# Full-height operands for two score products, closer softmax steps in layer B, a queries' product between two keys' products, and latent queries rotated by GpSimd

## The chip, the cores and the metric

The program runs on one core of one Trainium2 chip. Its metric is the device time of one execution in microseconds (us). The kernel before took 1611.77 us, the median of 3 runs (1610.45 to 1612.25). The engines are TensorE (PE, with its weight loads as PEld), VectorE (DVE), ScalarE (ACT), GpSimd (POOL) and SyncE (SP), which issues the loads.

## The reference, cut to what matters

Two blocks run one after the other over 512 tokens of width 1024. The first has a layer A (a stabilised mLSTM beside attention over a memory) and a layer B (latent attention with 8 heads beside memory attention); the second has differential attention, cross-attention over a second memory (layer D here) and an MLP. Two places of it matter here. In layer A the decay of a pair of tokens is exp(d - m_t), where m_t is the running maximum of a token:

```python
d = b[..., :, None] - b[..., None, :] + ib[..., None, :]
m_t = jnp.maximum(inter, jnp.max(d, axis=-1))
p = jnp.einsum("bhtd,bhsd->bhts", qb, kb) * jnp.exp(d - m_t[..., None])
```

In layer B each of 8 heads has queries and keys of 128 plain and 64 rotary components, normalised together; the rotary keys are shared by the heads but for each head's norm:

```python
q = (rmsnorm(q_lat, q_lat_g) @ w_q_up).reshape(bsz, s, B_HEADS, QK_HEAD)
q = rmsnorm(q, q_gain)
q = jnp.concatenate([q[..., :QK_NOPE], rope(q[..., QK_NOPE:], positions)], axis=-1)
...
sc = jnp.einsum("bqhd,bkhd->bhqk", q[:, qs:ke], k[:, :ke]) * scale
p = jax.nn.softmax(jnp.where(k_chunk <= q_chunk, sc, -jnp.inf), axis=-1)
```

In layer D, cross-attention, queries are `h @ w_cq` (512 tokens), keys and values `mem_n @ w_ckv` (256 tokens), with 4 heads of 256.

## The kernel before, in words

Every weight product is computed in three matmuls a tile, of a high and a low fp32r half of each operand (hi*hi, hi*lo, lo*hi). Weights come in chunks of 256 rows: SP loads a chunk into one of two raw slots (`fetch`), ACT copies its high half and DVE subtracts to get the low half (`split`), into one of three split slots. A product has 4 output tiles (banks 0 to 3), each evicted by ACT or DVE (`ev`). The attention scores, transposes and values are plain fp32 matmuls, in banks 4 to 7.

One list of steps sets the order on all engines. `order_of_work` calls `p.product(...)` for the products, and hangs side work (softmax units, transposes, values) into two lanes. `Plan.advance` takes the head of a lane between two product rows once a counted clock, which sums formula costs of PE's work, has moved on by that group's `lag` since the lane's last group. `rounds` makes the groups of an attention: group n holds the turn-over (transposes) of unit n-2, the normalising of unit n-1 and the scores of unit n, and `exp` of unit n stands in a group of its own after `wait`. Each engine's program walks the same list and runs the part that is its own, strictly in order.

The names that the change touches:

- `asc` is a score unit of layer B, one head and one block of 128 queries, 32 in all, 8 each of 128, 256, 384 and 512 keys. It is a matmul over the 128 plain components (L1404), one over the 64 rotary components (L1405; a head's half of the pair's rows is taken by `hs`) and a bf16 matmul that adds the mask (L1221). `atp` transposes the probabilities (L1205), `aval` multiplies them with the values (L1420). `msc`, `mtp`, `mval` are the same for the memory attention, 16 units in layer B.
- `hsc` is a score step of layer A, 16 in all: the running maximum is spread to 128 rows by a product with a 4-row selector (L1350), a mask is added, then come queries times keys (L1356, L1357).
- `latents(q)` prepares two heads: the products `kvB` and `quB`, then side steps `prep0` to `prep6`. `prep0`, `prep1`, `prep3`, `prep4` transpose the plain parts, `prep5` the rotary keys and `prep6` the rotary queries. DVE rotates the queries in `prep4` and `prep5`, with 7 instructions (recorded at the helper line L1927), and ACT moves the turned result of `prep6` from its bank into `peT`.
- GpSimd adds up the squares for norms (L2460), takes reciprocal roots (L2451) and does little else in layer B.
- `ckD0`, `ckD1` are the keys' products of layer D (256 tokens), `cqD0`, `cqD1` the queries', `cvD` the values'. `outB0`, `outB1` are the output product of layer B; its last tiles of input are the results of heads 4 to 7.

## Time and profile before

| what | value |
|---|---|
| median of 3 runs | 1611.77 us (1610.45 to 1612.25) |
| the profiled execution | 1605.89 us |
| its span, first to last instruction | 1604.1 us |
| mean granted TensorE clock | 0.993 of full speed |
| PE busy | 1552.2 us (97%) |
| DVE busy | 890.2 us (55%) |
| ACT busy | 705.5 us (44%) |
| POOL busy | 192.1 us (12%) |

Places in the span are given in us from its start. Layer B's attention lies at about 550 to 804 us, layer A's `hsc` steps at 168 to 390 us, layer D's products from 1068 us. A duration in a row of the timeline is from the first start to the last end of the instructions merged in it. Matmuls overlap in their records, so what a matmul costs TensorE is read from one start to the next. An fp32 product is recorded as two matmuls ("x2"), an fp32r product as one.

### The profile page before, as it was taken

What the parts mean: (1) busy time and instruction counts of PE and PEld (TensorE: products, weight loads), DVE (VectorE), ACT (ScalarE), POOL (GpSimd) and SP (SyncE); (2) the same over time, 40 slices, a digit from 0 to 9 for tenths busy, and PEclk for the clock granted to TensorE, in tenths of its full rate; (3) what the DMA queues carried; (4) which work ended last, traced back from release to release, by engine and by line L of the source; (5) the groups of instructions that cost most, each with busy time, mean ns of one, the idle gap of its engine ahead of it and who ended that gap; (6) DMA issues with size and microseconds to landing.
All of it is one profiled execution on the core that took longest, in us unless ns stands there. A gap on an engine that the chain in (4) does not pass through costs nothing.

```text
span 1604.1 us, 19197 instructions
## 1 busy us (share of the span) xinstructions
PE 1552.2 (97%) x7128; PEld 1239.7 (77%) x7128; DVE 890.2 (55%) x1775; ACT 705.5 (44%) x1607; POOL 192.1 (12%) x157
## 2 busy tenths in 40 slices
PE   7999999999999999999899999999999999999997
PEld 5887777777897877766478878688777888888886
DVE  6467485656465567556448557664455534444343
ACT  6544353333355666555334444442344333333241
POOL 3202020202120000000014004320001100000001
PEclk9999999999999999999999999999999999999998
DMA  5522122323424222121123321234322333333321
GB/s 191 158 74 72 53 80 66 92 66 118 125 67 143 81 62 61 49 71 42 40 79 120 92 67 55 65 105 120 99 84 79 95 103 93 101 96 93 105 93 65
DMA packets 89068, 141.04 MB, mean 88 GB/s; under 512 B 6416, under 2 KB 36496, under 8 KB 88976
## 3 DMA queue, kind: packets, MB, share of 16 engines
q1 hardware_dynamic: 88256, 139.02, 28.5%
q8 instruction: 56, 0.92, 0.2%
q10 hardware_dynamic: 720, 0.81, 0.1%
q14 instruction: 36, 0.29, 0.1%
HBM read 137.71 MB, written 2.10 MB: 87 GB/s over the span
## 4 chain that ended last, share of the span: by engine, by line
PE 78%; DVE 9%; ACT 5%; issue 3%; POOL 3%; DMA 2%; SPq 0%; POOLq 0%; ACTq 0%; DVEq 0%
PE banks L1242 16%; PE banks L1244 16%; PE banks L1243 16%; PE banks L1247 6%; PE banks L1249 6%; PE banks L1248 6%; PE banks L1205 2%; DVE sb_w_split L1927 2%; DVE sb_arena L1936 2%; ACT sb_junk L1512 2%; PE banks L1420 1%; PE banks L1405 1%; PE banks L1368 1%; ACT sb_w_split L1544 1%; DVE sb_arena L1927 1%
## 5 line engine op out<-in xcount | busy, mean ns | idle before, releaser
L1927 DVE TENSOR_TENSOR sb_w_split<-sb_raw,sb_w_split 128x512 fp32r<-128x512 f32 (+4 forms) x530 | 338.7, 681 | 359.8 <-ACT sb_w_split L1544 359.1
L1544 ACT ACTIVATE sb_w_split<-sb_raw 128x512 fp32r<-128x512 f32 (+4 forms) x530 | 288.2, 592 | 425.3 <-PE banks L1244 309.5
L1242 PE MATMUL banks<-sb_actA,sb_w_split 128*128 128x512 f32 x672 | 275.7, 410 | 0.3 <-ACT sb_arena L1604 0.3
L1244 PE MATMUL banks<-sb_actA,sb_w_split 128*128 128x512 f32 x672 | 262.7, 391 | 0.0
L1243 PE MATMUL banks<-sb_actA,sb_w_split 128*128 128x512 f32 x672 | 261.8, 390 | 0.0
L1242 PE MATMUL banks<-sb_actB,sb_w_split 128*128 128x512 f32 (+1 forms) x640 | 248.8, 389 | 4.2 <-DVE sb_actB L1927 2.2
L1244 PE MATMUL banks<-sb_actB,sb_w_split 128*128 128x512 f32 (+1 forms) x640 | 242.9, 379 | 0.0
L1243 PE MATMUL banks<-sb_actB,sb_w_split 128*128 128x512 f32 (+1 forms) x640 | 242.7, 379 | 0.0
L1247 PE MATMUL banks<-sb_w_split,sb_actA 128*128 128x512 f32 (+1 forms) x384 | 153.5, 400 | 12.6 <-DVE sb_w_split L1927 9.2
L1249 PE MATMUL banks<-sb_w_split,sb_actA 128*128 128x512 f32 (+1 forms) x384 | 149.3, 389 | 0.0
L1248 PE MATMUL banks<-sb_w_split,sb_actA 128*128 128x512 f32 (+1 forms) x384 | 149.0, 388 | 0.0
L1242 PEld LDWEIGHTS banks<-sb_actA,sb_w_split 128*128 128x128 f32 x672 | 126.4, 188 | 27.6 <-issue 2.9
L1244 PEld LDWEIGHTS banks<-sb_actA,sb_w_split 128*128 128x128 f32 x672 | 126.1, 188 | 27.6
L2460 POOL TENSOR_TENSOR sb_arena<-sb_arena 128x512 f32<-128x512 f32 x43 | 63.4, 1475 | 697.5 <-ACT sb_arena L1585 695.0
L1243 PEld LDWEIGHTS banks<-sb_actA,sb_w_split 128*128 128x128 f32 x672 | 126.5, 188 | 24.7 <-issue 0.7
L1242 PEld LDWEIGHTS banks<-sb_actB,sb_w_split 128*128 128x128 f32 x640 | 121.0, 189 | 27.7 <-DVE sb_actB L1927 2.7
L1243 PEld LDWEIGHTS banks<-sb_actB,sb_w_split 128*128 128x128 f32 x640 | 120.9, 189 | 22.9 <-issue 1.4
L1244 PEld LDWEIGHTS banks<-sb_actB,sb_w_split 128*128 128x128 f32 x640 | 120.7, 189 | 22.8
L2451 POOL TENSOR_TENSOR sb_small<-sb_small,sb_cons 128x4 f32<-128x4 f32 (+3 forms) x30 | 42.1, 1403 | 589.7 <-DVE sb_small L1933 589.7
L1247 PEld LDWEIGHTS banks<-sb_w_split,sb_actA 128*128 128x128 f32 x384 | 72.9, 190 | 26.9 <-issue 12.9
L1247 PE MATMUL banks<-sb_w_split,sb_actB 128*128 128x512 f32 (+2 forms) x208 | 81.5, 392 | 2.8 <-DVE sb_w_split L1927 1.7
L1249 PEld LDWEIGHTS banks<-sb_w_split,sb_actA 128*128 128x128 f32 x384 | 72.9, 190 | 14.5
(206 smaller groups left out, 2061.4 us busy)
## 6 DMA issues: line engine op xcount, KB each, us to landing
sb_raw<-in_a_w_in SPq DMA_DIRECT2D x66, 256.0 KB, 3.0
sb_raw<-in_w_up SPq DMA_DIRECT2D x32, 512.0 KB, 3.6
sb_raw<-in_w_down SPq DMA_DIRECT2D x32, 512.0 KB, 3.7
sb_raw<-in_w_in SPq DMA_DIRECT2D x24, 512.0 KB, 3.6
sb_raw<-in_mem_w_kv SPq DMA_DIRECT2D x16, 512.0 KB, 3.8
sb_raw<-in_w_ckv SPq DMA_DIRECT2D x16, 512.0 KB, 3.7
sb_raw<-in_a_w_in SPq DMA_DIRECT2D x15, 512.0 KB, 3.8
sb_raw<-in_a_w_out SPq DMA_DIRECT2D x12, 512.0 KB, 3.9
```

What stands on the lines that cost most here:

```text
L1205: t = pe.op.transpose(v.ps[0:rows, place.bank, n * P:(n + 1) * P], block, v.ident)
L1242: pe.op.matmul(out, hi[:, cs], x.hi(k), start=i == 0, stop=False)
L1243: pe.op.matmul(out, hi[:, cs], x.lo(k), start=False, stop=False)
L1244: t = pe.op.matmul(out, lo[:, cs], x.hi(k), start=False, stop=last_i)
L1247: pe.op.matmul(out, x.hi(k)[:, cs], hi, start=i == 0, stop=False)
L1248: pe.op.matmul(out, x.hi(k)[:, cs], lo, start=False, stop=False)
L1249: t = pe.op.matmul(out, x.lo(k)[:, cs], hi, start=False, stop=last_i)
L1512: t = act.op.activation(v.junk[:, 0:src.shape[-1]], src, ACT.Square, accum_out=out)
L1544: act.op.activation(hi[:, cs], raw[:, cs], ACT.Copy).then_inc(act.mark(m("w_hi"), 2 * n + part + 1), 1)
L1927: dve.op.tensor_tensor(out, a, b, op).then_inc(dve.mark(*mark) if mark else dve.tick(), 1)
L2451: pool.op.tensor_tensor(v.stat(root, n), v.stat(mean, n), v.con("minus_half", 0, n), ALU.pow).then_inc(m.at("rstd", step)[0], 1)
L2460: pool.op.tensor_tensor(total, total, v.square_of(norm, n)[1], ALU.add).then_inc(pool.mark(signal, value), 1)
```

## The change: what it does, and the diff

Seven edits, in three sorts. Full height: `m_rows` is a whole tile that GpSimd zeroes once and whose first 4 rows are `neg_m`, and L1350's product reads 128 rows of it. The rotary queries of each head go into a tile of their own, `q_pe`, whose other 64 rows are zeroed by GpSimd, so that the rotary product reads 128 rows; ACT's move in `prep6` becomes two of 64 rows each. Order: the `lag` and `wait` of the rounds in layer B are shorter, `prep6` stands further behind `prep5`, `ckD1` moves behind `cqD0`. Engine: the 7 instructions of `prep4` and `prep5` go from DVE to GpSimd.

```diff
@@ order_of_work: mla, mem_b, latents
-               lag=1400, wait=1000)
+               lag=1300, wait=1000)
...
-               [("hnscale", "mqB"), ("hnt", "mk1", 3)], [("silu", f"mzB{h0 // 2}", 1)], lag=1600, wait=1200)
+               [("hnscale", "mqB"), ("hnt", "mk1", 3)], [("silu", f"mzB{h0 // 2}", 1)], lag=1300, wait=1000)
...
-            p.side(1, [("asc", 2 * q - 3, TT - 1)] if q >= 2 and n == 0 else (), (f"prep{n}", q), lag=4000 if n in (0, 6) else 2600)
+            after = [("asc", 2 * q - 3, TT - 1)] if q >= 2 and n == 0 else [("ysplit", "yB", 3)] if (q, n) == (3, 4) else ()
+            p.side(1, after, (f"prep{n}", q), lag={0: 4000, 6: 6500}.get(n, 2600))
...
-    p.product("ckD1")
     p.rings = [(4, 5), (6, 7)]
     for g in range(2):
-        p.product(f"cqD{g}", [("nrow", "d")])
+        p.product(f"cqD{g}", [("nrow", "d")], first=False)
+        if g == 0:
+            p.product("ckD1")
@@ Views
-        self.neg_m = self.arena[0:4, at.at:at.at + SEQ]
-        at.take(SEQ)
+        self.m_rows = at.take(SEQ)
+        self.neg_m = self.m_rows[0:4, :]
...
+        self.q_pe = [[self.peT[n % 2][:, 1, :], other[n]] for n in range(4)]
@@ tensor_program
-            pe.op.matmul(mb, v.con("head_rows", h * P, (h + 1) * P, M_HEADS), v.neg_m[:, si * P:SEQ],
-                         start=True, stop=False)
+            pe.wait_ge(m("m_zero"), 1)
+            pe.op.matmul(mb, v.con("head_rows", h * P, (h + 1) * P), v.m_rows[:, si * P:SEQ], start=True, stop=False)
...
-            pe.op.matmul(s, eT[hs, 1, qs], eT[hs, 0, 0:ke], start=False, stop=False)
+            pe.wait_ge(m("q_fill"), (2, 4, 5, 6)[p])
+            pe.op.matmul(s, v.q_pe[p][hh][:, qs], eT[:, 0, 0:ke], start=False, stop=False)
@@ scalar_program, prep6
+                if s == 6:
+                    act.wait_ge(m("q_fill"), (2, 4, 5, 6)[p])
+                    act.op.activation(v.q_pe[p][0][0:64, :], src[0:64, :], ACT.Copy).then_inc(act.tick(), 1)
+                    t = act.op.activation(v.q_pe[p][1][64:P, :], src[64:P, :], ACT.Copy)
@@ evict_waits
+    if name == "zB3":
+        return [m.full(("asc", 3, TT - 1))]
@@ vector_program: prep4 and prep5 leave it
-                tensor(qs, qs, gq.unsqueeze(1).broadcast_to([P, TT, 2, QK_ROPE]), ALU.mult)
-                tensor(o1, s1, cos, ALU.mult)
-                tensor(o2, s2, cos, ALU.mult)
...
-                tensor(s1, s1, sin, ALU.mult)
-                tensor(s2, s2, sin, ALU.mult)
-                tensor(o1, o1, s2, ALU.subtract)
-                tensor(o2, o2, s1, ALU.add, *m.at("qp", step))
@@ gpsimd_program
+        elif kind in ("prep4", "prep5"):
+            pool.settle()
+            if kind == "prep4":
+                pool.wait_ge(*m.at("sums", ("prep3", n)))
+                if n:
+                    pool.wait_ge(*m.full(("prep6", n - 1)))
...
+                tensor(qs, qs, gq.unsqueeze(1).broadcast_to([P, TT, 2, QK_ROPE]), ALU.mult)
+                pool.settle()
+                tensor(o1, s1, cos, ALU.mult)
+                tensor(o2, s2, cos, ALU.mult)
+                continue
+            tensor(s1, s1, sin, ALU.mult)
+            tensor(s2, s2, sin, ALU.mult)
+            pool.settle()
+            tensor(o1, o1, s2, ALU.subtract)
+            tensor(o2, o2, s1, ALU.add, *m.at("qp", step))
+            pool.settle()
+            if n < 2:
...
+                pool.op.memset(v.q_pe[n][0], 0.0).then_inc(m("q_fill"), 1)
+            elif n == 2:
+                pool.wait_ge(*m.full(("msc", "B", MEM_HEADS - 1, TT - 1)))
+            else:
+                pool.wait_ge(*m.at("y_hi", ("ysplit", "yB", 3)))
+                pool.wait_ge(*m.at("y_lo", ("ysplit", "yB", 3)))
+            pool.op.memset(v.q_pe[n][1], 0.0).then_inc(m("q_fill"), 1)
```

What the new distances do to TensorE's order shows at the end of layer B. Before, this is what stands from the second score unit of head 6 on (L1205 turns probabilities, L1404, L1405 and L1221 are a score unit, L1420 a head's values; the rows end before the values of head 7):

```order
L1405 MATMUL banks<-sb_arena 128x256
L1221 MATMUL banks<-sb_masks 128x128
L1205 MATMUL banks<-sb_cons,sb_arena 128x128
L1404 MATMUL banks<-sb_arena 128x384
L1405 MATMUL banks<-sb_arena 128x384
L1221 MATMUL banks<-sb_masks 128x128
L1205 MATMUL banks<-sb_cons,sb_arena 128x128 x2
L1404 MATMUL banks<-sb_arena 128x512
L1405 MATMUL banks<-sb_arena 128x512
L1221 MATMUL banks<-sb_masks 128x128
L1205 MATMUL banks<-sb_cons,sb_arena 128x128 x3
```

Now, in the changed kernel (4 lines further down: L1209, L1408, L1410, L1225; L1246 to L1248 are the matmuls of product `outB0`), from the mask of the same second unit of head 7 on:

```order
L1225 MATMUL banks<-sb_masks 128x128
L1246 MATMUL banks<-sb_actB,sb_w_split 128x512
L1247 MATMUL banks<-sb_actB,sb_w_split 128x512
L1248 MATMUL banks<-sb_actB,sb_w_split 128x512
L1425 MATMUL banks<-sb_arena 128x512
L1425 MATMUL banks<-sb_arena 128x384
L1425 MATMUL banks<-sb_arena 128x256
L1425 MATMUL banks<-sb_arena 128x128
L1209 MATMUL banks<-sb_cons,sb_arena 128x128
L1408 MATMUL banks<-sb_arena 128x384
L1410 MATMUL banks<-sb_arena 128x384
L1225 MATMUL banks<-sb_masks 128x128
```

Before, the units of heads 6 and 7 follow each other with nothing between them from the second one on, and only 8 rows of `outB0` are left behind them, since the others have been used up. Now the units up to the second of head 7 have 4 rows (12 matmuls) of `outB0` between them, and only the last two units of head 7 stand bare.

On GpSimd the steps of layer B were a row of reciprocal roots:

```order
L2451 TENSOR_TENSOR sb_small<-sb_small,sb_cons 128x4 x3
L2451 TENSOR_TENSOR sb_small<-sb_small,sb_cons 128x8
L2451 TENSOR_TENSOR sb_small<-sb_small,sb_cons 128x16
L2451 TENSOR_TENSOR sb_small<-sb_small,sb_cons 128x8 x8
L2460 TENSOR_TENSOR sb_arena<-sb_arena 128x512 x4
```

In the changed kernel the same roots (L2449 there) have the rotation (L2441) and the zeroing between them:

```order
L2449 TENSOR_TENSOR sb_small<-sb_small,sb_cons 128x8 x2
L2441 TENSOR_TENSOR sb_arena<-sb_arena,sb_rows 128x8x64
L2441 TENSOR_TENSOR sb_arena<-sb_arena 128x8x32 x6
L2513 MEMSET sb_arena 128x512
L2519 MEMSET sb_arena 128x512
L2449 TENSOR_TENSOR sb_small<-sb_small,sb_cons 128x8 x2
```

So each of the four pairs of heads has 7 elementwise instructions and one or two memsets on GpSimd, behind the two roots of the pair and ahead of the next pair's.

## Rows read from the trace of the kernel before

**Rows 1.** The page, part 1: busy time, share of the span, instructions.

```profile
PE 1552.2 (97%) x7128; PEld 1239.7 (77%) x7128; DVE 890.2 (55%) x1775; ACT 705.5 (44%) x1607; POOL 192.1 (12%) x157
```

**Rows 2.** Timeline, TensorE, a score unit of layer B: start, length, line, form.

```profile
645.61 1.02 PE L1404 MATMUL banks<-sb_arena 128*128 128x512 f32 x2
646.56 1.12 PE L1405 MATMUL banks<-sb_arena 64*128 64x512 f32 x2
647.62 0.23 PE L1221 MATMUL banks<-sb_masks 128*128 128x128 bf16 x1
```

**Rows 3.** Timeline, TensorE, a full-height score product of the second block.

```profile
935.68 1.02 PE L1436 MATMUL banks<-sb_arena 128*128 128x512 f32 x2
936.54 0.22 PE L1221 MATMUL banks<-sb_masks 128*128 128x128 bf16 x1
```

**Rows 4.** Timeline, TensorE, the 4-row product of layer A behind a product row.

```profile
167.68 0.39 PE L1248 MATMUL banks<-sb_w_split,sb_actA 128*128 128x512 f32 x1
167.91 0.39 PE L1249 MATMUL banks<-sb_w_split,sb_actA 128*128 128x512 f32 x1
168.22 1.12 PE L1350 MATMUL banks<-sb_arena,sb_cons 4*128 4x512 f32 x2
169.28 0.23 PE L1221 MATMUL banks<-sb_masks 128*128 128x128 bf16 x1
```

**Rows 5.** Who waited for whom, TensorE, 560 to 775.5: total, times, longest.

```profile
PE banks L1205 <- DVE sb_arena L1930: 3.3, 2, 3.0
PE banks L1205 <- DVE sb_actB_plain L1930: 2.6, 2, 1.4
...
PE banks L1242 <- DVE sb_actB L1927: 0.7, 1, 0.7
```

**Rows 6.** The same view, 775.9 to 804.5 us, all of it.

```profile
PE banks L1205 <- DVE sb_arena L1930: 5.5, 4, 2.4
PE banks L1242 <- DVE sb_actB L1927: 1.5, 1, 1.5
PE banks L1420 <- ACT sb_arena L1807: 0.8, 1, 0.8
```

**Rows 7.** Timeline, all engines, 726 to 735: the longest wait of layer B.

```profile
726.65 2.18 ACT L1758 ACTIVATE sb_actB<-sb_arena 128x512 fp32r<-128x512 f32 x4
...
729.78 0.44 ACT L1690 ACTIVATE sb_arena<-banks,sb_small 128x128 f32<-128x128 f32 x1
...
734.15 0.33 PE L1205 MATMUL banks<-sb_cons,sb_arena 128*128 128x128 f32 x1 [3.05 <-DVE sb_arena L1930]
```

**Rows 8.** Timeline around 790, turning the second and the last unit of head 7.

```profile
791.68 0.44 PE L1205 MATMUL banks<-sb_cons,sb_arena 128*128 128x128 f32 x2 [0.88 <-DVE sb_arena L1930]
...
796.91 0.66 PE L1205 MATMUL banks<-sb_cons,sb_arena 128*128 128x128 f32 x4 [2.38 <-DVE sb_arena L1930]
```

**Rows 9.** Timeline, layer D: DVE alone, and beside GpSimd.

```profile
1069.18 0.74 DVE L1936 SCALAR_TENSOR_TENSOR sb_actA<-sb_x_res,sb_cols,sb_actA 128x512 fp32r<-128x512 f32 x1
...
1070.99 3.01 POOL L2460 TENSOR_TENSOR sb_arena<-sb_arena 128x512 f32<-128x512 f32 x2 [2.60 <-ACT sb_arena L1585]
...
1071.04 3.51 DVE L1936 SCALAR_TENSOR_TENSOR sb_actA<-sb_x_res,sb_cols,sb_actA 128x512 fp32r<-128x512 f32 x2
```

**Rows 10.** Groups by form: GpSimd over the span, DVE 620 to 800.

```profile
L2460 POOL TENSOR_TENSOR sb_arena<-sb_arena 128x512 f32<-128x512 f32 x43 | 63.4, 1475 | 697.5 <-ACT sb_arena L1585 695.0 <-POOL sb_arena L2460 0.3
L2451 POOL TENSOR_TENSOR sb_small<-sb_small,sb_cons 128x8 f32<-128x8 f32 x10 | 17.8, 1784 | 200.9 <-DVE sb_small L1933 200.9
L1927 DVE TENSOR_TENSOR sb_arena<-sb_arena 128x256 f32<-128x256 f32 x18 | 6.9, 422 | 0.3
```

**Rows 11.** Timeline, layer D: the second keys' product starts late.

```profile
1082.98 0.36 PE L1242 MATMUL banks<-sb_actB,sb_w_split 128*128 128x256 f32 x1 [2.07 <-DVE sb_arena L1927]
```

**Rows 12.** Stretches: length, busy PE, PEld, DVE, ACT, POOL, PEclk, DMA, GB/s.

```profile
797.70:801.10 3.40, 2.75 (x4) 1.44 (x5) 0.00 (x0) 0.50 (x1) 0.00 (x0) 0.51 0.00 0
1084.50:1087.90 3.40, 3.40 (x19) 3.40 (x18) 0.86 (x2) 0.65 (x2) 0.00 (x0) 0.50 0.71 222
```

More of the change, by code:

```diff
@@ L920, in __init__ @@
         self.zT = [two[:, 1, 0:2, :], at.take(2, SEQ), two[:, 1, 4:6, :], Layout(self.arena, ARENA - 2048).take(2, SEQ)]
+        other = [self.zT[3][:, 0, :], self.zT[3][:, 1, :], two[:, 0, 6, :], self.zT[1][:, 0, :]]
+        self.q_pe = [[self.peT[n % 2][:, 1, :], other[n]] for n in range(4)]
         mprob_b = two[:, 0, 0:2, :].rearrange("p a b -> p (a b)")
@@ L2123, in vector_program @@
             dve.settle()
+            dve.wait_ge(m("m_zero"), 1)
             scalar(v.neg_m, g[3], -1.0, ALU.mult)
@@ L2282, in vector_program @@
             rk4 = v.stat(("kr", p), 2 * TT).rearrange("p (i h) -> p i h", h=2).unsqueeze(3)
-            qs = v.q_raw.rearrange("p i (h n) -> p i h n", h=2)[:, :, :, P:]
-            qd = v.pair_pe[:, 1, :, :].rearrange("p i (h n) -> p i h n", h=2)
-            s1, s2, o1, o2 = qs[:, :, :, 0:HALF], qs[:, :, :, HALF:], qd[:, :, :, 0:HALF], qd[:, :, :, HALF:]
-            cos, sin = (w.unsqueeze(2).broadcast_to([P, TT, 2, HALF]) for w in (v.cosB, v.sinB))
             if s == 1:
@@ L2306, in vector_program @@
                        rk4.broadcast_to([P, TT, 2, QK_ROPE]), ALU.mult, *m.at("kp", step))
-            elif s == 4:
-                gq = v.rows[:, ROW["q_gain_pe"]:ROW["q_gain_pe"] + 128].rearrange("p (h n) -> p h n", h=2)
-                dve.wait_ge(*m.at("sums", ("prep3", p)))
-                tensor(qs, qs, gq.unsqueeze(1).broadcast_to([P, TT, 2, QK_ROPE]), ALU.mult)
-                dve.settle()
-                tensor(o1, s1, cos, ALU.mult)
-                tensor(o2, s2, cos, ALU.mult)
-            elif s == 5:
-                dve.settle()
-                tensor(s1, s1, sin, ALU.mult)
-                tensor(s2, s2, sin, ALU.mult)
-                dve.settle()
-                tensor(o1, o1, s2, ALU.subtract)
-                tensor(o2, o2, s1, ALU.add, *m.at("qp", step))
             elif s == 6:
@@ L2444, in gpsimd_program, with tensor @@
     pool = Stream(engine, m, "pool_own")
+    def tensor(out, a, b, op, *mark):
+        pool.op.tensor_tensor(out, a, b, op).then_inc(pool.mark(*mark) if mark else pool.tick(), 1)
     pool.wait_ge(m("dma_cons"), 16)
@@ L2490, in gpsimd_program @@
                                       ALU.mult).then_inc(m("gw_zero"), 1)
+            pool.wait_ge(*m.at("sq_sum", ("sqp", "mem", 3)))
+            pool.op.memset(v.m_rows, 0.0).then_inc(m("m_zero"), 1)
             for u in range(4):
```

18 lines of the change are left out of this document (15 added, 3 removed).

## The prediction, on record before the changed kernel ran

> **What bounds the kernel now.** I read the page's part 1 first: TensorE is busy 97% of the span [rows 1], so a change pays only by what it takes from TensorE's own work or from the 3% in which it stands. The timeline of TensorE, read from start to start, gives the price of each matmul; the view of who waited for whom gives what it stands for, by stretch. In layer B it waits 3.3 + 2.6 + 0.7 = 6.6 us from 560 to 775.5 in the groups shown, the longest wait 3.0 [rows 5], and 5.5 + 1.5 + 0.8 = 7.8 us in the 28 us from 775.9 on [rows 6]. That is 14.4 us, most of it for DVE's normalising of a softmax unit. The other two sources to look at are the TensorE clock, which shows 0.5 (1.2 GHz) in two short stretches near this work [rows 12], and a single wait in layer D [rows 11].
>
> **Full height.** A score unit of 512 keys goes from its plain product (start 645.61) to its rotary product (646.56) in 0.95 us, and from there to the mask (647.62) in 1.06 [rows 2]. A full-height fp32 product of the same 512 columns, 935.68 to 936.54, takes 0.86 [rows 3]. So the plain product is 0.09 dearer and the 64-row one 0.20, 0.29 a unit. Both are explained by one thing: each recorded matmul that stands before or in the 64-row product costs about 0.1 more. The plain product is full height and as wide as the reference, and still pays, so the extra sits at the step between two matmuls and not in the columns. With zeros in the other 64 rows every operand is full height and the columns are the same, so I take all of it: 32 x 0.29 = 9.3 us. Were it in proportion to columns (a mean of 320 of 512), it would be 5.8.
>
> The 4-row product of layer A shows the same: 168.22 to 169.28 is 1.06, so 0.20 too dear, and the matmul ahead of it has 0.31 to the next start where the one before had 0.23, so 0.08 more [rows 4]. 16 x 0.28 = 4.5 us; at 5/8 of that, 2.8. Together 13.8 us, from 8.6 on if columns count. All of it lies on TensorE, which is the bound there, and nothing hides it. The zeroing costs TensorE nothing: `m_rows` is filled long before gate results exist, and its wait is one for a thing done.
>
> On this the Trainium skill speaks against the change: "TensorE: Matmul & The Clock Gate", Part 3, under "What overlaps and what doesn't", says that a weight load overlaps with running matmuls only when its row group differs. By that rule equal heights would put each load in the open, and the change would lose time (the second rival below has the price from rows). The trace does not agree: the full-height product of rows 3 is the quicker one, though all its loads have the same rows.
>
> **Rotation on GpSimd.** Four times, 7 instructions leave DVE (one of 512 elements, six of 256, at 0.42 [rows 10], so some 3 us a pair) and come to GpSimd. There 512 elements take 1.48 us [rows 10]; for 256 I take half, 0.74, with 1.48 as the upper bound. That is 1.48 + 6 x 0.74 = 5.9 us a pair (upper 10.4), behind a root of 1.78 [rows 10] that stands ahead of it: 7.7 us (12.2) from the last sum of squares to the rotated queries. What waits for them is `prep6` on TensorE. Its distance from `prep5` rises, and by the order there stand 16 or more product rows between `prep3` and `prep6` of a pair, each of three matmuls with some 0.2 us a step (0.23 at 512 columns [rows 4]), 10 us, besides four score units of 2.0 us at most [rows 2], with the mean width 5 us. ACT's squares take a few us of that. So the nominal chain is hidden, and the upper one only just. Queued behind it on GpSimd are the next pair's roots, a whole pair away. ACT gets one more short copy a pair, beside TensorE's work.
>
> What it does cost is DVE's time: beside GpSimd two DVE instructions that take 0.74 alone took 3.51 together, 1.75 each [rows 9]. GpSimd will be busy 4 x 5.9 = 24 us more in layer B, and DVE's normalising and splitting in these windows is late by up to an instruction of GpSimd each. DVE also has 12 us less to do. A turn-over meets such a delay in perhaps two groups a pair: 8 x 0.25 = 2 us lost. Bounds: 0 (all covered), and 8 x 1.0 = 8 (as long a hold as in rows 9, never covered).
>
> The Trainium skill's "SBUF — State Buffer", section "SBUF: two separate sides", calls the shared pair of ports an exclusive lock, where the later of the two blocks for the whole instruction. Rows 9 fit that. By that rule the upper bound of 8 us is the nearer one if DVE mostly comes second; the sum above keeps 2.
>
> **Order in layer B.** The longest wait, 3.05 us at 734.15, is the first transposes of head 4: ACT copied four high halves at 726.65, 2.18 us long, then split a chunk, and its exponential came only at 729.78 [rows 7]. Now that unit stands in `zB3`, before those four copies, and has been normalised by then; what follows them has 7 rows of `outB0` and a head's values to cover it. I count the 3.0 as gone. The end: before, heads 6 and 7 have their units bare from the second one on, and wait 5.5 us for DVE in 4 places [rows 6]. Now 4 rows of `outB0` stand between them up to the second unit of head 7. Its last two keep theirs, 0.88 and 2.38 [rows 8]; 5.5 - 3.3 = 2.2 goes. The values of head 7 (0.8) and the last rows of `outB0` behind them (1.5) wait as before, since the chain from head 7's last unit is as it was [rows 6]. The 0.7 in rows 5 is `outB0`'s fifth tile, asked for right after head 5; now 20 rows lie between, and it goes. In sum 3.0 + 2.2 + 0.7 = 5.9 us. The 2.6 us in 2 waits at the memory attention [rows 5] I leave as they are: its units now come every 3 rows, 9 x 0.23 = 2.1 us, in place of 4 to 5, so some waits go and some come. Bounds of the whole term: a gain of 6.6 + 2.2 = 8.8 (all but the bare end goes) and a loss of 2.6 (nothing goes, and the memory units wait twice as long). Less the 2 us of GpSimd, layer B gives 3.9 us.
>
> **Layer D.** `ckD0` is followed by `cqD0` in place of `ckD1`. The wait of 2.07 us [rows 11] is at the first matmul behind `ckD0`: its bank is evicted by DVE only after a late split. That queue is the same with `cqD0` behind it, so the wait stays. Afterwards nothing waited before, and now two short products no longer follow each other. The value is 0, bounds 2.1 gained and, with one such wait more, 2.1 lost. The clock was 0.50 from 1084.5, after this wait, and 0.51 from 797.7, after the 2.38 of the bare end [rows 12]. A stretch of 3.4 us at half clock gives 1.7 us back if it does not come. Both waits stay, so I count none; it is a spread of 1.7 either way, for each.
>
> **The sum.** 13.8 + 3.9 = 17.7 us. The profiled execution took 1605.9 us with a span of 1604.1; it would take 1588.2. The median of runs is 1611.8, 5.9 above it, and I carry the difference over: 1594.1 us.
>
> **Rivals.** *The zeros buy nothing*: the extra belongs to the rotary and stabiliser products as such. For it: the two are also those with a mask behind them. Against it: rows 3 have a mask behind them too. Gain 3.9, time 1607.9. *Loads in the open*: each full-height matmul pays its load, which I price from rows 2 at the 0.1 that a step costs, for every record of such a unit (4 of `asc`, 2 of `hsc`) on top of the 0.52 of today: 128 x 0.1 + 32 x 0.1 = 16 us lost, less 3.9 gained: 1623.9. Rows 3 speak against it. *Layer B's order gives nothing*, or GpSimd's hold on DVE eats it: 13.8 less 2 is 11.8, time 1600.0. For it: DVE's queue is strict and the units come closer. *More goes*: the waits outside the bare end vanish (8.8 us instead of 5.9), GpSimd costs nothing, one stretch of half clock goes (1.7) and so does layer D's wait (2.1): 13.8 + 8.8 + 3.8 = 26.4, time 1585.4. *Slower*: the closer units in layer B outrun the chain from maximum to exponential to normalising, at every transpose of its 48 units, because DVE is held by GpSimd and ACT by the squares. It decides from 13.8 / 48 = 0.29 us more a unit on. At the 1.0 us of a hold as in rows 9 it costs 48 us: 1611.8 - 13.8 + 48 = 1646. Against it: GpSimd's new work is 24 us in some 250 of layer B, and in the uncovered end the same chain made TensorE wait 0.88 to 2.38, while 12 x 0.23 = 2.8 us of rows now stand there [rows 4, 8].
>
> **How the numbers follow.** The forecast, 1594.1 with its own range of 1588 to 1600, has 0.60. Order gives nothing 0.16, more goes 0.14, zeros buy nothing 0.05, loads in the open 0.01, slower 0.04. The range for 8 in 10 reaches from 1584 to 1603: it holds the forecast, the 1600 and the 1585.4, and leaves out the other three and the outer part of that last case. No change (within 0.2%, 3.2 us, about what a measurement can tell) needs the zeros to fail and most of the order too: 0.02. Faster has 0.93, slower 0.05.
>
> **What would show it.** Right: a unit's rotary product 0.86 us at 512 keys and the plain one ahead of it 0.86; L1350's successor the same; no wait of 3 us near head 4; at the end one wait of some 2.4, one of 0.9; rotation instructions on GpSimd of 0.7 to 0.8 us, and none of TensorE's waits at `prep6`. Wrong: a full-height rotary product at 1.06; half-width GpSimd instructions of 1.5 us and TensorE waiting for them; waits on L1930's successor at many units of layer B; half clock inside layer B.

## The result, and the profile after

The changed kernel took 1584.91 us, the median of 4 executions (1583.33 to 1587.18), beside 1611.11 us for the kernel before (1609.57 to 1612.25): a ratio of 0.9839, interval 0.9822 to 0.9856, 26.2 us less. The forecast was 1594.1; the result lies below its own range of 1588 to 1600 and inside the range for 8 in 10, 1584 to 1603. One execution of the kernel before, in a later series, took 2229.3 us at a mean clock of 0.654 and is left out of every median and ratio here. The profiled executions stand nearer to it: 1605.89 us before and 1586.22 after, 19.7 us less, where the sum had 17.7. So two things are to be explained: 2 us in the sum, and 7 us between the profiled executions and the medians. (The prediction worked with 1611.77, the median of the first 3 executions.)

In the page's part 1, [rows 1] have become:

```profile
PE 1535.1 (97%) x7128; PEld 1245.0 (79%) x7128; DVE 887.2 (56%) x1747; ACT 707.6 (45%) x1611; POOL 223.0 (14%) x192
```

TensorE has the same number of matmuls and is busy for 17.1 us less. In the timeline of TensorE, a score unit of 512 keys, the answer to [rows 2], and the stabiliser product of layer A, the answer to [rows 4]:

```profile
629.54 1.02 PE L1408 MATMUL banks<-sb_arena 128*128 128x512 f32 x2
630.41 1.02 PE L1410 MATMUL banks<-sb_arena 128*128 128x512 f32 x2
631.26 0.22 PE L1225 MATMUL banks<-sb_masks 128*128 128x128 bf16 x1
...
168.42 0.40 PE L1253 MATMUL banks<-sb_w_split,sb_actA 128*128 128x512 f32 x1
168.65 1.02 PE L1355 MATMUL banks<-sb_arena,sb_cons 128*128 128x512 f32 x2
169.51 0.22 PE L1225 MATMUL banks<-sb_masks 128*128 128x128 bf16 x1
```

From start to start the plain product now takes 0.87 and the rotary one 0.85, against 0.95 and 1.06; L1355 takes 0.86 against 1.06, and the step ahead of it 0.23 against 0.31.

The first of the column sums that begin the next norm mark the ends of layer B in both kernels. Their rows in the timeline, after (L1279) and before (L1275):

```profile
458.39 0.95 PE L1279 MATMUL banks<-sb_cons,sb_arena 128*128 128x1 f32 x8
...
837.52 1.02 PE L1279 MATMUL banks<-sb_cons,sb_arena 128*128 128x1 f32 x8 [1.00 <-POOL sb_arena L2458]
```

```profile
462.53 0.95 PE L1275 MATMUL banks<-sb_cons,sb_arena 128*128 128x1 f32 x8
...
855.92 1.02 PE L1275 MATMUL banks<-sb_cons,sb_arena 128*128 128x1 f32 x8 [1.00 <-POOL sb_arena L2460]
```

Up to the first mark the changed kernel is 4.1 us shorter, layer B is 379.1 in place of 393.4, 14.3 shorter, and what follows is shorter by 1.3 more. Who waited for whom on TensorE, first from 447.4 to 745 (the largest groups) and then from 745 to 827 us, in the changed kernel (total, times, longest), the answer to [rows 5, 6]:

```profile
PE banks L1209 <- DVE sb_actB_plain L1941: 6.0, 6, 1.7
PE banks L1209 <- DVE sb_arena L1941: 3.0, 5, 1.1
...
PE banks L1209 <- DVE sb_arena L1941: 3.6, 2, 2.2
PE banks L1246 <- DVE sb_actB L1938: 1.5, 1, 1.5
PE banks L1425 <- ACT sb_arena L1816: 0.8, 1, 0.8
```

The wait of 3.0 near head 4 [rows 7] is gone. The bare end has 3.6 us in 2 waits for DVE in place of 5.5 in 4. The memory attention (sb_actB_plain) waits 6.0 us in place of 2.6 [rows 5]. In the table of stretches, two that answer to [rows 12]; the seventh figure is the granted clock:

```profile
779.70:783.10 3.40, 3.40 (x6) 1.68 (x7) 0.00 (x0) 0.00 (x0) 0.00 (x0) 0.51 0.02 5
1064.60:1068.00 3.40, 3.40 (x19) 2.98 (x20) 2.07 (x5) 1.39 (x3) 0.00 (x0) 1.00 0.53 162
```

Half clock still comes at the bare end, but not behind layer D's wait, which is 2.1 us long as before [rows 11]. That is the 1.7 us there.

On GpSimd the rotation of the first pair, from the timeline (start, length), and its groups by form over the span:

```profile
595.97 2.00 POOL L2449 TENSOR_TENSOR sb_small<-sb_small,sb_cons 128x8 f32<-128x8 f32 x1 [8.28 <-DVE sb_small L1944]
597.94 1.66 POOL L2441 TENSOR_TENSOR sb_arena<-sb_arena,sb_rows 128x512 f32<-128x512 f32 x1
599.68 5.09 POOL L2441 TENSOR_TENSOR sb_arena<-sb_arena 128x256 f32<-128x256 f32 x6
```

```profile
L2441 POOL TENSOR_TENSOR sb_arena<-sb_arena 128x256 f32<-128x256 f32 x24 | 21.9, 935 | 0.9
L2449 POOL TENSOR_TENSOR sb_small<-sb_small,sb_cons 128x8 f32<-128x8 f32 x10 | 17.9, 1789 | 166.4 <-DVE sb_small L1944 166.4
```

A half-width instruction takes 0.94 us in the mean, where the prediction had 0.74 (the 24 range from 0.72 to 1.28, so 0.74 is what the quickest take); the chain with its root is 8.8 us in place of 7.7, and nothing in the waits above names it.

### The profile page after: what moved, and what is told of

Read it like the earlier page. It is cut to its first block, busy times and chain, and to the rows that moved or that the text cites. A ratio compares the mean times of both kernels' runs of the same rounds, so it can differ in the third digit from the quotient of the medians.

```text
span 1584.4 us, 19220 instructions
## 1 busy us (share of the span) xinstructions
PE 1535.1 (97%) x7128; PEld 1245.0 (79%) x7128; DVE 887.2 (56%) x1747; ACT 707.6 (45%) x1611; POOL 223.0 (14%) x192
## 4 chain that ended last, share of the span: by engine, by line
PE 78%; DVE 9%; ACT 5%; issue 3%; POOL 3%; DMA 2%; SPq 0%; POOLq 0%; ACTq 0%; DVEq 0%
PE banks L1246 16%; PE banks L1248 16%; PE banks L1247 16%; PE banks L1251 6%; PE banks L1253 6%; PE banks L1252 6%; DVE sb_w_split L1938 2%; PE banks L1209 2%; DVE sb_arena L1947 2%; ACT sb_junk L1517 2%; PE banks L1372 1%; ACT sb_w_split L1549 1%; PE banks L1425 1%; PE banks L1488 1%; DVE sb_arena L1941 1%
## 5 line engine op out<-in xcount | busy, mean ns | idle before, releaser
L1938 DVE TENSOR_TENSOR sb_w_split<-sb_raw,sb_w_split 128x512 fp32r<-128x512 f32 (+4 forms) x530 | 344.4, 692 | 365.5 <-ACT sb_w_split L1549 364.8
L1246 PE MATMUL banks<-sb_actA,sb_w_split 128*128 128x512 f32 x672 | 276.4, 411 | 2.4 <-DVE sb_arena L1938 2.1
L1248 PE MATMUL banks<-sb_actA,sb_w_split 128*128 128x512 f32 x672 | 263.1, 392 | 0.0
L1246 PE MATMUL banks<-sb_actB,sb_w_split 128*128 128x512 f32 (+1 forms) x640 | 248.5, 388 | 1.5 <-DVE sb_actB L1938 1.5
L1248 PE MATMUL banks<-sb_actB,sb_w_split 128*128 128x512 f32 (+1 forms) x640 | 242.9, 380 | 0.0
L2458 POOL TENSOR_TENSOR sb_arena<-sb_arena 128x512 f32<-128x512 f32 x43 | 63.4, 1474 | 686.5 <-ACT sb_arena L1590 684.1
L1246 PEld LDWEIGHTS banks<-sb_actA,sb_w_split 128*128 128x128 f32 x672 | 126.5, 188 | 32.3 <-issue 7.2
L1248 PEld LDWEIGHTS banks<-sb_actA,sb_w_split 128*128 128x128 f32 x672 | 126.2, 188 | 27.3
L1246 PEld LDWEIGHTS banks<-sb_actB,sb_w_split 128*128 128x128 f32 x640 | 120.6, 188 | 26.1 <-issue 2.5
L1248 PEld LDWEIGHTS banks<-sb_actB,sb_w_split 128*128 128x128 f32 x640 | 120.5, 188 | 22.8
L2449 POOL TENSOR_TENSOR sb_small<-sb_small,sb_cons 128x4 f32<-128x4 f32 (+3 forms) x30 | 42.1, 1404 | 548.9 <-DVE sb_small L1944 548.9
```

The source lines that it names most:

```text
L1246: pe.op.matmul(out, hi[:, cs], x.hi(k), start=i == 0, stop=False)
L1248: t = pe.op.matmul(out, lo[:, cs], x.hi(k), start=False, stop=last_i)
L1938: dve.op.tensor_tensor(out, a, b, op).then_inc(dve.mark(*mark) if mark else dve.tick(), 1)
L2449: pool.op.tensor_tensor(v.stat(root, n), v.stat(mean, n), v.con("minus_half", 0, n), ALU.pow).then_inc(m.at("rstd", step)[0], 1)
L2458: pool.op.tensor_tensor(total, total, v.square_of(norm, n)[1], ALU.add).then_inc(pool.mark(signal, value), 1)
```

## The experiments

Each ran in 4 to 8 executions beside the kernel before, whose median was between 1610.7 and 1611.6 us in every series. "Clock" is the mean granted clock of the executions.

| kernel | median us | ratio to before, interval | clock |
|---|---|---|---|
| changed | 1584.9 | 0.9839, 0.9822 to 0.9856 | 0.994 |
| full height alone | 1593.7 | 0.9888, 0.9872 to 0.9903 | 0.993 |
| changed, 4 and 64 rows again | 1598.1 | 0.9916, 0.9903 to 0.9928 | 0.993 |
| changed, all distances of before | 1598.8 | 0.9923, 0.9911 to 0.9936 | 0.991 |
| changed, rotation on DVE | 1585.0 | 0.9839, 0.9825 to 0.9852 | 0.993 |
| changed, layer D's order of before | 1588.1 | 0.9855, 0.9837 to 0.9872 | 0.993 |
| changed, `prep6` near | 1585.5 | 0.9845, 0.9824 to 0.9866 | 0.993 |
| both score products on 64 rows | 1595.4 | 0.9901, 0.9884 to 0.9918 | 0.992 |
| changed, softmax distances of before | 1595.8 | 0.9904, 0.9889 to 0.9919 | 0.991 |
| changed, memory attention further | 1586.4 | 0.9854, 0.9839 to 0.9869 | 0.992 |
| the same, heads nearer | 1592.1 | 0.9883, 0.9868 to 0.9899 | 0.990 |
| changed, a split later in layer D | 1584.9 | 0.9834, 0.9818 to 0.9849 | 0.994 |
| the kernel before, once more | 1610.1 | 0.9998, 0.9983 to 1.0014 | 0.989 |

### Full height alone, and everything but full height

The first of two runs is the changed kernel with the distances, layer D's order and the rotation put back, here in part:

```diff
-               lag=1300, wait=1000)
+               lag=1400, wait=1000)
...
+            elif s == 4:
+                gq = v.rows[:, ROW["q_gain_pe"]:ROW["q_gain_pe"] + 128].rearrange("p (h n) -> p h n", h=2)
...
```

> The kernel before with the full-height operands alone (zeroed rows for the 4-row product of layer A and the 64-row product of layer B); the distances, layer D and the rotation on DVE are as before. Theory (each recorded matmul in or next to a partial-height one costs 0.09 to 0.10 us more, 9.6 us in layer B and 4.5 in layer A): 14.1 us less than before, 1597.0 us; 42 to 462 us of the span shorter by 4.3, layer B shorter by 9.6. Rival one (order and engine gave most of it): 5 us less, 1606. Rival two (the 6 us by which the medians differ more than the profiled executions belong to the zeros): 20 us less, 1591.

The second is the changed kernel with the two products back at their old heights:

```diff
-            pe.op.matmul(mb, v.con("head_rows", h * P, (h + 1) * P), v.m_rows[:, si * P:SEQ], start=True, stop=False)
+            pe.op.matmul(mb, v.con("head_rows", h * P, (h + 1) * P, M_HEADS), v.neg_m[:, si * P:SEQ], start=True, stop=False)
...
-            pe.op.matmul(s, v.q_pe[p][hh][:, qs], eT[:, 0, 0:ke], start=False, stop=False)
+            pe.op.matmul(s, v.q_pe[p][hh][hs, qs], eT[hs, 0, 0:ke], start=False, stop=False)
```

> The changed kernel with the two products back at 4 and 64 rows, reading the same tiles; zeroing, order and engines stay as changed. Theory: the 14.1 us come back, 1599.0 us, with the same 0.29 to 0.30 a unit at every width, since the cost is fixed a step. Rival (cost in proportion to the columns, a mean of 5/8): 0.30 at 512 keys and 0.07 at 128, 8.8 us in all, 1593.7. Rival (the zeros gain only where the order leaves no waits): under 8 us.

Alone, full height took 17.5 us off (1593.7, against 1597.0 expected). Taken out of the changed kernel it costs 13.2 us (1598.1, against 1599.0 expected). The profile of the second, in the timeline of TensorE, has a unit of 512 and one of 128 keys:

```profile
635.73 1.02 PE L1408 MATMUL banks<-sb_arena 128*128 128x512 f32 x2
636.69 1.12 PE L1411 MATMUL banks<-sb_arena 64*128 64x512 f32 x2
637.74 0.23 PE L1225 MATMUL banks<-sb_masks 128*128 128x128 bf16 x1
...
641.39 0.39 PE L1408 MATMUL banks<-sb_arena 128*128 128x128 f32 x2
641.71 0.49 PE L1411 MATMUL banks<-sb_arena 64*128 64x128 f32 x2
642.12 0.23 PE L1225 MATMUL banks<-sb_masks 128*128 128x128 bf16 x1
```

At 512 keys the two steps are 0.96 and 1.05, at 128 keys 0.32 and 0.41; at full height a 128-key unit of the changed kernel has 0.22 and 0.22 (634.90, 635.12 and 635.34 in its timeline). So it is 0.09 and 0.20 at 512 keys, 0.10 and 0.19 at 128. The price is fixed, not in proportion to columns: 32 x 0.30 = 9.6 us in layer B, 16 x 0.28 = 4.5 us in layer A, 14.1 in all. Not all of it comes back in the time: TensorE's waits in layer B (447 to 848 us) sum to 14.5 us in that profile and to 16.4 in the changed kernel's, so some 2 us of dear steps only fill what were waits.

### What in the height costs

The rotary product is on 64 rows again, and now the plain product on the same 64; layer A's product is on 96. The plain product thereby leaves out half of its components, so this kernel only measures a price:

```diff
-            pe.op.matmul(s, nT[:, 2 + hh, qs], nT[:, hh, 0:ke], start=True, stop=False)
+            pe.op.matmul(s, nT[hh * 64:hh * 64 + 64, 2 + hh, qs], nT[hh * 64:hh * 64 + 64, hh, 0:ke], start=True, stop=False)
...
+            pe.op.matmul(mb, v.con("head_rows", h * P, (h + 1) * P, 96), v.m_rows[0:96, si * P:SEQ], start=True, stop=False)
```

> A measurement of the step price, not a version: the changed kernel with both of layer B's score products on the same 64 rows (the plain product leaves out the other 64 of its components, and the rotary one the zeros), and layer A's stabiliser product on 96 rows. Theory (a step is dearer by 0.09 to 0.10 when the matmul on either side of it is of partial height): five dear steps a unit, 0.50 more than at full height, 16 us more in layer B; 96 rows cost as 4 and 64 did, 4.5 us in layer A; in all 20.5, 1605.5 us. Rival one (what costs is the change from one height to another): the steps between the two partial products are cheap, two or three dear ones stay, 0.2 to 0.3 a unit, 9 us in layer B. Rival two (the price falls with the rows that are used): 96 rows nearly as cheap as 128.

The theory failed, twice: it took 1595.4 us, 10.5 more than the changed kernel, where the theory had 20.5 more and the first rival 9. Its profile, in the timeline of TensorE: a unit of 512 keys with the transposes ahead of it, then layer A's product on 96 rows.

```profile
631.20 0.38 PE L1209 MATMUL banks<-sb_cons,sb_arena 128*128 128x128 f32 x2
631.51 1.12 PE L1408 MATMUL banks<-sb_arena 64*128 64x512 f32 x2
632.47 1.02 PE L1411 MATMUL banks<-sb_arena 64*128 64x512 f32 x2
633.42 0.23 PE L1225 MATMUL banks<-sb_masks 128*128 128x128 bf16 x1
...
168.72 0.40 PE L1253 MATMUL banks<-sb_w_split,sb_actA 128*128 128x512 f32 x1
168.96 1.02 PE L1355 MATMUL banks<-sb_arena,sb_cons 96*128 96x512 f32 x2
169.82 0.22 PE L1225 MATMUL banks<-sb_masks 128*128 128x128 bf16 x1
```

The two products on 64 rows take 0.96 and 0.95. Taken apart into single matmuls (medians of all units of 512 keys, from one start to the next), with the transpose ahead of the unit first and the mask last:

| | transpose | plain 1 | plain 2 | rotary 1 | rotary 2 | mask |
|---|---|---|---|---|---|---|
| all 128 rows | 109 | 432 | 430 | 428 | 429 | 29 ns |
| rotary on 64 | 109 | 432 | 522 | 533 | 522 | 38 ns |
| both on 64 | 202 | 533 | 429 | 429 | 522 | 39 ns |

With both on 64 rows the steps between them cost what full height costs. What is dear is to go from one height to another: 0.09 in the step ahead of the first matmul of the other height, 0.10 in the one behind it, 0.09 on the way back and 0.01 in the mask's own step, 0.30 for going and returning, with two matmuls between or with four. And 96 rows are no other height: 0.24 to its start and 0.86 to the mask, as with 128, while 4 and 64 rows both paid.

The weight loads show what is paid. In the timeline of PEld, first the two loads of the rotary product and the mask's in the changed kernel, then in the kernel with 64 rows:

```profile
629.98 0.19 PEld L1410 LDWEIGHTS banks<-sb_arena 128*128 128x128 f32 x1 [0.24 <-issue]
630.41 0.19 PEld L1410 LDWEIGHTS banks<-sb_arena 128*128 128x128 f32 x1 [0.24 <-issue]
...
636.68 0.29 PEld L1411 LDWEIGHTS banks<-sb_arena 64*128 64x128 f32 x2 [0.76 <-issue]
637.74 0.10 PEld L1225 LDWEIGHTS banks<-sb_masks 128*128 128x128 bf16 x1 [0.76 <-issue]
```

At equal height the first load of the rotary product starts at 629.98, with the matmul ahead of it and 0.43 before its own (630.41). At 64 rows it starts only at 636.68, where its own matmul stands (636.69), and so does the mask's, at 637.74: the load of another height is not put under the running matmul. Layer A shows it too: the load for 96 rows starts at 168.73, 0.23 before its matmul, the one for 4 rows with its matmul (168.22 in the kernel before).

This is a rule that the prediction did not weigh. The Trainium skill, "TensorEngine Tiling (Array Packing)", section "Tiling Modes", lists the array whole, in two halves of 64 rows and in four of 32, and says that changing the mode drains TensorE. If 4 and 64 rows are run in such a mode and 96 in the whole one, which no row here states, that rule fits what the rows above show; it gives no price, and the runs give 0.30 us.

### The distances

The first run puts all three back in the changed kernel, the second the lags and waits, the third `prep6` alone:

```diff
-               lag=1300, wait=1000)
+               lag=1400, wait=1000)
-                [("hnscale", "mqB"), ("hnt", "mk1", 3)], [("silu", f"mzB{h0 // 2}", 1)], lag=1300, wait=1000)
+                [("hnscale", "mqB"), ("hnt", "mk1", 3)], [("silu", f"mzB{h0 // 2}", 1)], lag=1600, wait=1200)
-            p.side(1, after, (f"prep{n}", q), lag={0: 4000, 6: 6500}.get(n, 2600))
+            p.side(1, after, (f"prep{n}", q), lag={0: 4000, 6: 4000}.get(n, 2600))
```

> The changed kernel with layer B's distances of before (1400 and 1000 for the heads, 1600 and 1200 for the memory attention, 4000 for prep6). Theory (the distances are worth what the waits show: 3.0 near head 4 and 2 at the end, less 3.4 that the memory attention waits more): 2 to 5 us more, 1588.5, the wait of 3 us back, the memory attention's waits back to 2.6 us. Rival (what the layer gained beyond the zeros came from relieving DVE of the rotation): no change, 1585. Rival (the closer steps cost more than they give): 2 us less, 1583.

> The changed kernel with only the distances of the softmax steps put back (1400 and 1000 for the heads, 1600 and 1200 for the memory attention); prep6 keeps its 6500. Theory: the distances are worth what lies between the full-height kernel and the one with rotation on DVE, 8.7 us, so 1593.7 or a little under; the wait of 3 us near head 4 back, 1.4 to 2 us more at the end, 3 us less at the memory attention, so 2 to 3 us of waits and the rest in stretches of half clock. Rival (the distance of prep6 is what made the difference): within 2 us of the changed kernel, 1586.

> The changed kernel with the rotated queries' transposes at the distance of before (4000 in place of 6500), with the rotation still on GpSimd. Theory (GpSimd's chain of root and seven instructions is 6.4 to 6.9 us, longer than the near distance covers; that is the 3.4 us wait seen when all distances were put back): TensorE waits for GpSimd by some 3 us at one pair or more, a stretch of half clock may follow: 3 to 6 us more, 1589. Rival (the near distance is enough when the other steps are closer, and the wait belonged to the wider ones): 1585.

With all three back the kernel took 13.9 us more, where I had expected 2 to 5. The distances of the softmax steps alone are worth 10.9 us (1595.8, against 1593.7 expected), the largest single part of the order. With these put back, TensorE's waits from 447 to 840 us show (the largest groups):

```profile
PE banks L1209 <- DVE sb_arena L1941: 10.0, 7, 3.4
PE banks L1209 <- DVE sb_actB_plain L1941: 3.4, 4, 1.4
PE banks L1246 <- DVE sb_actB L1938: 2.4, 2, 1.4
PE banks L1425 <- ACT sb_arena L1816: 1.7, 3, 0.8
PE banks L1209 <- DVE sb_arena L1938: 1.2, 2, 0.6
```

All its groups there sum to 21.7 us against 16.4 in the changed kernel, 5.3 more. The mean clock of the executions is 0.991 against 0.994, which at the 1.1 us for each 0.001 found below is some 3 us (an estimate). The 2 us or so that are left have no cause shown. Behind the wait of 3.4 (head 4, at 723.9) and behind the bare end the stretches were:

```profile
724.50:727.90 3.40, 3.40 (x9) 1.80 (x9) 1.85 (x4) 1.40 (x4) 3.24 (x5) 0.59 0.00 0
785.40:792.20 6.80, 5.82 (x13) 3.63 (x14) 0.21 (x2) 0.60 (x1) 0.00 (x0) 0.50 0.00 0
```

`prep6` by itself is worth nothing (1585.5, overlapping with the changed kernel). With the old lags it is worth 3.0 us (1598.8 against 1595.8), and there GpSimd's chain shows. In the timeline of the kernel with all distances of before, GpSimd and then TensorE:

```profile
680.76 4.97 POOL L2441 TENSOR_TENSOR sb_arena<-sb_arena 128x256 f32<-128x256 f32 x6
...
685.78 1.54 PE L1209 MATMUL banks<-sb_cons,sb_arena 128*128 128x128 f32 x6 [3.43 <-POOL sb_arena L2441]
```

So my expectation for `prep6` was wrong: whether the near distance is too near is decided by what else stands between.

### The engine of the rotation

The 7 instructions of `prep4` and `prep5` go back to `vector_program`; GpSimd keeps the zeroing:

```diff
-        elif kind in ("prep4", "prep5"):
+        elif kind == "prep5":
```

> The changed kernel with the 7 rotation instructions of each pair back on DVE; GpSimd keeps only the zeroing. Theory (what GpSimd holds back on DVE and what DVE is relieved of are both covered, since in the profile no wait stands by the rotation): within 1 us, 1585. Rival (GpSimd holds DVE at turn-overs): 2 us less, 1583. Rival (DVE's relief is what made the closer steps possible): 3 or more us more, 1588, with waits for DVE's normalising in each pair.

1585.0 against 1584.9: nothing to be told apart. Both prices are there and both are covered. In the groups by form from 540 to 790 us, DVE's low halves of 512 elements, first with the rotation on GpSimd and then on DVE, take 742 and 688 ns, 24 x 0.054 = 1.3 us of DVE's time:

```profile
L1938 DVE TENSOR_TENSOR sb_w_split<-sb_raw,sb_w_split 128x512 fp32r<-128x512 f32 x24 | 16.8, 742 | 14.3 <-ACT sb_w_split L1549 14.3
```

```profile
L1938 DVE TENSOR_TENSOR sb_w_split<-sb_raw,sb_w_split 128x512 fp32r<-128x512 f32 x24 | 15.5, 688 | 13.9 <-ACT sb_w_split L1549 13.9
```

This is only one form of several. The low halves of 384 elements take 878 in place of 552 ns (8 of them, two of 1.32 us), and over all forms that both kernels have DVE is busy 8.1 us longer in that window beside GpSimd, against the 12.9 us that the rotation took off it. TensorE's waits in layer B sum to 16.4 us with GpSimd and 15.7 without, so DVE's lateness hardly reaches TensorE. The 2 us that I had charged were not paid.

### Layer D

The first run takes the order of before. The second keeps the changed one and has one split later:

```diff
-            while self.n_split <= n + self.ahead - 1:
+            last = c == len(pr.order) - 1
+            while self.n_split <= n + self.ahead - 1 - (name == "ckD0" and last):
```

> The changed kernel with layer D's second keys' product back right behind the first and the queries' products after both. Theory (the 2 us wait is the same in both orders, and only a stretch of half clock behind it came or went by chance): within 1 us of the changed kernel, 1585.0; the wait of 2.0 to 2.1 us again at the first matmul behind the first keys' product. Rival (the changed order is what kept the clock up there): 1.7 us more, and half clock at about 1065 us of the span in the profile.

> The changed kernel with one split of a weight chunk put behind the evictions of layer D's first keys' product, on DVE and ACT, in place of ahead of them (its load moves with it). Theory (the 2.1 us wait there is DVE standing at a late split with the evictions queued behind it): the wait goes, 2.1 us less, 1582.8, and with it the half clock that follows it in some runs. Rival (the late load only moves the wait to the first matmul that needs that chunk): no change, the wait by the split in place of the eviction.

With the order of before the median is 3.2 us higher, where I had expected at most 1, but the intervals overlap. Its profile has the same wait at the same place, 2.4 us long, and half clock behind it (mean 0.69 from 1065.5 to 1068.9); whether the order or chance brings that stretch is open. The later split does what it should. In the timeline of TensorE, where 2.14 us stood, there is now no wait:

```profile
1063.35 0.28 PE L1249 MATMUL banks<-sb_actB,sb_w_split 128*128 128x256 f32 x1
```

From that norm's column sums to the next ones (the 1058.48 and 1232.06 of the changed kernel) it is 171.2 us in place of 173.6. The median did not follow (1584.9, against 1582.8 expected); its executions spread from 1581.95 to 1586.26 with clocks of 0.996 to 0.991, so a gain of 2 us is in the mechanism and not shown in the time.

### Wider for the memory, nearer for the heads

The first run changes the memory attention's line alone, the second both:

```diff
-               lag=1300, wait=1000)
+               lag=1200, wait=900)
-                [("hnscale", "mqB"), ("hnt", "mk1", 3)], [("silu", f"mzB{h0 // 2}", 1)], lag=1300, wait=1000)
+                [("hnscale", "mqB"), ("hnt", "mk1", 3)], [("silu", f"mzB{h0 // 2}", 1)], lag=1500, wait=1100)
```

> The changed kernel with the memory attention's distances at 1500 and 1100 and the heads' left at 1300 and 1000. The rows of the output product between the units of heads 6 and 7 stay as they are; only the memory units stand further apart. Theory (the changed kernel's waits at the memory attention, 6.0 us in 6, come from its shorter distances alone): they fall to 2 to 3.5 us, the rest of layer B's waits stay, 3 us less, 1582. Rival (the units are late through DVE, whatever the distance): no change, 1585. Rival (the later start of the heads costs the cover at the end): 3 us more.

> As the version with the memory attention at 1500 and 1100, and the heads at 1200 and 900. Now 5 rows of the output product stand between the units up to the last of head 7, 2 behind it. Theory (a unit waits when fewer rows stand between it and its normalising than the chain needs): the wait of 1.4 at the end goes, the 2.2 shrinks by 2 rows or 1.4 us, while the heads' closer units wait 1 to 2 us more at heads 2 to 4: 1 to 2 us less than that version, 1580.5. Rival (the closer units wait at most turn-overs): 0.3 us each at 32, 8 us more, 1590.

Neither beat the changed kernel: 1586.4 and 1592.1, where I had expected 1582 and 1580.5. The memory attention's waits fell only from 6.0 to 4.8 us, one of them now 2.4 us long and with half clock at its end, and small waits elsewhere, the longest of 1.0 us, took some of it back. With the heads nearer, 9 rows of the output product stand behind the units from the second of head 7 on (4, 4 and 1), where the changed kernel has 1, and the end still waits, in the timeline of TensorE:

```profile
678.26 0.66 PE L1209 MATMUL banks<-sb_cons,sb_arena 128*128 128x128 f32 x4 [2.30 <-DVE sb_arena L1941]
...
780.61 0.66 PE L1209 MATMUL banks<-sb_cons,sb_arena 128*128 128x128 f32 x4 [3.36 <-DVE sb_arena L1941]
```

One wait of 3.4 replaced waits of 1.4 and 2.2, and a new one of 2.3 came at the earlier heads. The rows that now stand ahead of the last unit are missing behind it, where its chain has only 1 row to hide in. The rival that had the time nearly right (1590) had waits at most turn-overs, and they are not there: there are 5 waits for the heads' normalising, not 32.

### The kernel before, once more, with no edit

> The kernel before, unchanged, profiled once more. The execution that the prediction was summed against shows a mean clock of 0.993 and 1605.9 us; most others of the kernel showed 0.987 to 0.990 and 1609 to 1613. Theory (the difference of 5.9 us between that execution and the median is not a fixed cost but stretches of half clock, 1.7 us each, that come in some executions and not in others): an execution at 0.988 shows 5 to 8 us more lost at half clock than the profiled one's 5 us, with the same waits of TensorE; the stretches lie behind waits in layers B and D, at about 727, 790, 1006 and 1085 us. Rival (the difference lies in waits for loads or at the start): the same stretches and longer waits.

This execution took 1612.3 us at a mean clock of 0.988. TensorE's waits are nearly those of the first profile ([rows 5, 6, 7, 11] have 3.0 and 2.07); three of its groups over the span:

```profile
PE banks L1205 <- DVE sb_arena L1930: 10.8, 8, 3.0
PE banks L1205 <- DVE sb_actB_plain L1930: 2.6, 2, 1.4
PE banks L1242 <- DVE sb_arena L1927: 2.3, 1, 2.3
```

But layer B took 399.1 us in place of 393.4, and its table of stretches has three of 6.8 us at half clock (seventh figure), where the first profile had one of 3.4 [rows 12] and full clock from 735.5 to 742.5:

```profile
735.50:742.50 7.00, 7.00 (x20) 4.08 (x19) 4.17 (x12) 3.00 (x8) 0.60 (x1) 0.57 0.00 0
789.80:796.60 6.80, 6.80 (x16) 3.52 (x14) 1.41 (x5) 1.28 (x5) 0.00 (x0) 0.53 0.00 0
803.60:810.40 6.80, 5.52 (x14) 3.34 (x15) 0.52 (x2) 0.70 (x2) 0.00 (x0) 0.54 0.00 0
```

Each begins at the end of a wait of TensorE, in its last 1.1 us or the 0.5 us after it: of 3.04 us (to 735.07, head 4), of 1.58 (788.90) and of 2.38 (804.10, both in the bare end). At half clock for 3 x 6.8 us, up to 10.2 us are lost in place of 1.7; layer B is longer by 5.7, since part of the stretches falls into waits, and all waits of the layer sum to 18.9 in place of 20.0. So the 5.9 us between the profiled execution and the median of the kernel before are half clock, and not a fixed cost.

The other executions agree. Over 45 of the kernel before, with mean clocks from 0.985 to 0.993, a straight line gives 1.1 us more for each 0.001 less of mean clock, with a scatter of 1.2 us. The clocks of the 14 profiles show which waits are followed: the wait of 2.9 to 3.0 us at 141 us is in all 14, with half clock at its end in 9; the 3.0 to 3.4 us near head 4 in 5, followed in 3; the bare end of layer B has a stretch in 13 of 14.

## Why the prediction was right, and where it was not

**Full height, 13.8 us: right in size, wrong in cause.** The runs show 14.1 at full clock. I put the price on each recorded matmul before or in the 64-row product; the runs put it on the change of height, where the next weights are not loaded under the running matmul. Here the two give the same, since each unit went and returned once. "Loads in the open" is excluded, and is the wrong way round: full-height loads start with the matmul ahead of them (629.98), against the rule on row groups that the prediction takes from the Trainium skill ("TensorE: Matmul & The Clock Gate", Part 3), and it is the load of another height that stands in the open (636.68). "The zeros buy nothing" is excluded by two runs.

**Order in layer B, 5.9 us less 2 for GpSimd: near in the sum by luck.** The two waits that I had named went as named: the 3.0 is gone, and the end fell from 5.5 to 3.6 us (I had 3.3). The memory attention, which I had left at 2.6 us, waits 6.0. Put together the waits fell from 20.0 to 16.4, by 3.6, a little under the 3.9 that I had. But two terms were wrong and nearly cancel: the memory attention lost 3.4 us where I had 0, and GpSimd's hold, for which I had charged 2, cost TensorE at most 0.7 (16.4 against 15.7). Layer B's profiled gain beyond full height is 14.3 - 9.6 = 4.7.

**Layer D, 0.** The wait stayed, as said; a stretch of half clock did not come back in that profile, 1.7 us.

**The step that missed** is "the median of runs is 1611.8, 5.9 above it, and I carry the difference over". In the changed kernel the profiled execution is not 5.9 under the median but 1.3 over it. These 7.2 us are nearly all of the 9.2 by which the forecast was high. I had treated half clock as a spread of 1.7 us around two waits that I knew from one execution, and its effect on the median as a fixed cost. The later series show that this execution (0.993) is at the upper end, with 0.988 in most others, so the median holds several stretches more. From 0.989, the mean of the kernel before, to 0.994 the line of 1.1 us for 0.001 gives some 6 us (an estimate), most of the 7.2. That each long wait that goes takes one chance of a stretch with it fits the profiles and is argued, not tested by itself. It is part of why the distances are worth 10.9 us in the medians and 5.3 in the waits, and of why full height alone gave 17.5 and not 14.1. Why fewer dear steps should leave the clock up more often is not settled: full height took no wait away, and that the 3 us are clock follows only from the mean clocks, 0.993 against 0.988.

Of the rivals, "more goes" (1585.4) was met in time by luck, by another way: half clock in place of the waits and layer D's wait that it counted.

## What to carry to other kernels

An fp32 product on 4 or 64 rows between products on 128 cost 0.28 to 0.30 us for the two changes of height, the same at 128 and at 512 columns: pad it with zeros (96 rows were enough), or put several such products together, as four matmuls in a row paid no more than two. Where one profiled execution has a higher mean clock than the others, sum against it, but add what the others lose at half clock, and count each wait of TensorE of 2 to 3 us as that wait and a chance of up to 1.7 or 3.4 us behind it (less, where the stretch falls into further waits). A distance between steps is worth what stands between them in the whole order: moved alone, `prep6` did nothing, and with the older lags the same move was worth 3 us.

## What was not expected of the hardware

- Of the heights tried, 4 and 64 rows pay 0.28 and 0.30 us for going and returning, 96 rows pay nothing. The load of the other height starts with its own matmul (636.68), that of the same height with the matmul ahead (629.98).
- Between two fp32 products that both read the same 64 rows the next weights load under the running matmul as at full height (the load of L1411 starts at 632.04, its matmul at 632.47; 429 ns a step at 512 columns, 0.11 at 128).
- Stretches of half clock are 3.4 or 6.8 us long, begin at the end of a wait of TensorE (in its last 1.1 us or within 1.7 us after it, all 47 in the 14 profiles but for the end of the span), and come in one execution and not in the next with the same waits: in the 45 executions of the line above and the profiled one the same kernel showed mean clocks from 0.985 to 0.993 and 1605.9 to 1616.6 us.
- GpSimd takes 0.94 us in the mean for a product of 256 elements beside DVE (0.72 to 1.28), and 1.47 for 512 (L2458, 1.28 to 1.84). In turn DVE was busy 8.1 us longer beside 28 such instructions, and TensorE's waits rose by 0.7.
